# One change in six parts to an encoder block with routed experts: order of small matmuls, one rstd chain, a refill in two halves, a bias moved, stores on two queues

## The chip, the cores and the metric

The kernel runs on one core of one Trainium2 chip. The metric is the device time of one execution in microseconds (us); lower is better. The engines are TensorE (PE, with its weight loads as PEld), VectorE (DVE), ScalarE (ACT), GpSimd (POOL) and SyncE (SP), whose queue issues nearly all transfers.

## The reference, cut to what matters

One layer of an encoder on x (256 tokens, 1024 features, float32). The part around the change is the end of the first sub-layer, the routed experts and the final norm:

```python
x = x + gate1 * (merged @ w_mix_out)                      # this is x1 in the kernel
h = rms_norm(x, norm_ffn_g) * (1 + scale2) + shift2
logits = h @ w_router + b_router                          # 32 experts
top_val, top_idx = lax.top_k(logits, 4); gates = softmax(top_val)
# for each expert e, on its tokens:
gu = h[toks] @ w_gate_up[e] + b_gate_up[e]                # 1024 x 2048
gate = min(gu[:, :1024], 7); up = clip(gu[:, 1024:], -7, 7)
y = ((up + 1) * gate * sigmoid(1.702 * gate)) @ w_down[e] + b_down[e]
x = x + gate2 * sum over the token's 4 experts of gates * y
out = rms_norm(x, final_norm_g)
```

Everything is float32. The weights of the 32 experts are 12 MiB each (8 for gate and up, 4 for down), and all of them are read once.

## The kernel before, in words

The 256 tokens lie as two tiles (t = 0, 1) of 128 rows. Each engine has its own hand-written program, and the engines meet at counting semaphores: an engine's queue is worked off in order, so what stands behind a wait waits too.

**Weights.** A pair is two experts, A and B, of 64 token slots each. It reads twelve blocks of 2 MiB: four for gate and up of A, two for down of A, four for gate and up of B, two for down of B. The blocks go through eleven slots in SBUF in turn (place, L342). SP issues the loads (L403 gate and up, L409 down); before each it waits in free (L434) until PE has counted, on the semaphore consumed, the block that lay in the slot. Fifteen pairs (FIXED) are written out, the last goes through a loop whose count comes from a table (looped_pair), and its last down block is loaded as four halves of 1 MiB (L467). Block 11 of the first pair is the first refill: it goes into slot 0, which held gate-and-up block 0 of the same pair, and waits for that block's count. The three loads ahead of it wait for the mixing matmuls and for x1.

**Between the mixing product and the experts.** On DVE, residual (L1555) makes x1 in five pieces and counts x1_rdy; the last piece is columns 768 to 1023 of tile 1. ACT squares the rows of x1 (L1187). row_rstd (L1574) turns the sums of one tile into 1/sqrt(mean) by a chain of nine small steps, for tile 0 ahead of the last residual piece, for tile 1 at the end. PE turns x1 over (L796), multiplies it with the router weights (L801), puts in the gate-and-up biases (L834), and adds x1 to the accumulators with an identity matrix (add_x1, L829: four matmuls of 512 columns, tiles and halves apart). Three of those stand ahead of the first gather: two before the ranks (L839 to L841), which wait for m01_rdy from DVE, and one after them. DVE answers the ranks with the selection matrices (L1602); PE then gathers the tokens of pair 0 (L854), ACT and DVE scale them (L1205, L1618), and gate_up_block (L892, sixteen records a block) starts. The fourth add_x1 follows the four blocks.

**A pair on PE.** gate_up(A), scatter of the pair before (L923), act_transpose (L904, waits for DVE's activation L1656 to L1660), ACT's copy (L1217), down (L916), gate_up(B), gather of the next pair (L880), down (B). In DVE, y_copy (L1698) scales the product of down and counts y_rdy.

**The end.** After pair 14 comes down_bias (L970: four matmuls of 512 columns with 32 rows), then the looped pair, whose first instruction waits for y_rdy of the pair before; then the last scatter. ACT squares (L1259), DVE multiplies with the final gain (L1803), runs the rstd chain for both tiles (L1811, L1289 to L1297), ACT scales tile 0 (L1263), DVE tile 1 (L1814, L1816), and SP stores the four quarters of the output (L485).

Of the kernel before, what the change touches and what calls it, by code (L numbers as in the profile page):

```python
# [29 lines left out]
ALU = mybir.AluOpType  # L30
# [3 lines left out]
P = 128  # L34
D = 1024
L = 256
TT = L // P
# [63 lines left out]
def build(nc, a, out):  # L101
    with ExitStack() as ctx:
# [39 lines left out]
        NJ, NC = 4, 2  # L142
# [112 lines left out]
        def sem(name):  # L255
# [9 lines left out]
            s_ps s_sb negm_rdy exp_done a_rdy aT_ps aT_sb o_ps o_sq on_rdy oT_ps oT_sb  # L265
            rb_ps rb_sb pj_ps pj_sb gat_rdy mix_ps x1_rdy x2_rdy x1_sq  x1T_ps bc_sb x1T_dve x1T_act exc_sb
            log_ps top_rdy top_exp m_rdy rank_ps cnt_ps cnt_sb ex_ps g_all gt_ps gt_sb tables sel0_rdy m01_rdy ga0_act ga0_dve
            consumed tr_done sc_done ga_done pt_done
            g_rdy sig_rdy act_rdy actT_rdy y_rdy ga_sb pt_sb sel_rdy wt_rdy mask_rdy
            sc_part fin_sq fin_rs fin_act fin_rdy loop_y dve_step act_step dve_loop pool_step""".split()  # L270
        S = {n: sem(n) for n in names}
# [63 lines left out]
        FIXED = E // 2 - 1  # L335
# [28 lines left out]
        def _(sp):  # L364
# [69 lines left out]
            def free(p, i):  # L434
                sp.wait_ge(S["consumed"], used(p, i - NS + 1))
# [34 lines left out]
            def expert_of(index):  # L470
                return sp.value_load(table_i[0:1, bass.ds(index, 1)], min_val=0, max_val=E - 1)

            free(0, DB + 1)
            down(place(0, DB + 1), 1, 1)
            for p in range(1, FIXED):
# [7 lines left out]
            sp.dma_start(fgB, a["final_norm_g"][:].partition_broadcast(P)).then_inc(S["fg_in"], 16)  # L483
            def store(t, h):
                sp.dma_start(out[0, t * P:(t + 1) * P, 512 * h:512 * (h + 1)], fin[:, t, 512 * h:512 * (h + 1)])\  # L485
                    .then_inc(S["out_done"], 16)

            sp.wait_ge(S["fin_act"], 1)
            store(0, 0)
            sp.wait_ge(S["fin_rdy"], 1)  # L490
            store(1, 1)
            sp.wait_ge(S["fin_act"], 2)
            store(0, 1)
            sp.wait_ge(S["fin_rdy"], 2)
            store(1, 0)
            sp.wait_ge(S["out_done"], 16 * TT * 2)

# [11 lines left out]
        def _(pe):  # L509
# [318 lines left out]
            def add_x1(t, h):  # L828
                mm(bank(2 * t + h), ident, x1[:, t, h * 512:(h + 1) * 512], start=True, stop=False, skip_group_check=True)  # L829
# [15 lines left out]
            biases(0)  # L845
            add_x1(1, 0)
            add_x1(1, 1)
            pe.wait_ge(S["m01_rdy"], 1)
            ranks(0, M01).then_inc(S["rank_ps"], 1)
            add_x1(0, 0)  # L850

# [32 lines left out]
            def gate_up_block(p, s, j):  # L884
                w, landed, count = place(p, (A0, B0 if isinstance(p, int) else L_B)[s] + j)
                pe.wait_ge(landed, count)
                for kk in range(2):
                    k = 2 * j + kk
                    for b in range(2):
                        for h in range(2):  # L890
                            o = kk * 2048 + b * 1024 + h * 512
                            last = mm(ps[64 * h:64 * h + 64, 4 + b, :], hTp[:, k, s * 64:(s + 1) * 64],  # L892
                                      w[:, o:o + 512], start=False, stop=(k == KD - 1))
                last.then_inc(S["consumed"], 1)

# [47 lines left out]
            for j in range(NJ):  # L943
# [10 lines left out]
                elif j == 1:  # L954
                    expert_sums()
            pe.wait_ge(S["exc_sb"], 1)
            add_x1(0, 1)

# [27 lines left out]
            def down_b(p):  # L986
                pe.wait_ge(S["ga_sb"], p * 2 + 1)
                pe.wait_ge(S["act_rdy"], p * 2 + 2)
                act_transpose()
                pe.wait_ge(S["actT_rdy"], p * 2 + 2)  # L990
                pe.wait_ge(S["wt_rdy"], p + 1)
                place_weights()
                pe.wait_ge(S["ga_sb"], p * 2 + 2)
                down([place(p, DB + c) for c in range(NC)])

            down_a(0)
            gate_up_b(0)
            down_b(0)

            def pair_of(p):  # L1000
                pe.wait_ge(S["mask_rdy"], p + 1)
                gate_up(p, 0)
                pe.wait_ge(S["y_rdy"], p * 2)
                pe.wait_ge(S["pt_sb"], p)
                scatter()
                down_a(p)
                gate_up_b(p)
                down_b(p)

            for p in range(1, FIXED):  # L1010
                pair_of(p)
            down_bias()

# [35 lines left out]
        def _(act):  # L1049
# [212 lines left out]
            for h in range(2):  # L1262
                A(fin[:, 0, 512 * h:512 * (h + 1)], fin[:, 0, 512 * h:512 * (h + 1)], ACT.Copy, scale=rs[:, 0:1])\  # L1263
                    .then_inc(S["fin_act"], 1)

        @block.vector
        def _(v):
# [304 lines left out]

            def row_rstd(t):  # L1574
                v.wait_ge(S["x1_sq"], 2 * t + 2)
                step(V.tensor_tensor(ss[:, t:t + 1], ss4[:, 2 * t:2 * t + 1], ss4[:, 2 * t + 1:2 * t + 2], ALU.add))
                rstd1(rs[:, t:t + 1], ss[:, t:t + 1], D)

            row_rstd(0)
            residual(1, 768, 256, 5, 5)  # L1580
            columns_in(1, 2)
            row_rstd(1)

# [255 lines left out]
```

## Time and profile before

| what | value |
|---|---|
| three runs | 1218.56, 1224.4, 1225.47 us; median 1224.4 |
| the profiled execution | 1226.03 us; its span in the profile 1224.2 us |
| PE busy | 1135.1 us, 93% of the span |
| DVE busy | 426.7 us, 35% |
| ACT busy | 152.2 us, 12% |
| weights and inputs read | 463.77 MB, 380 GB/s over the span |
| mean granted TensorE clock | 0.987 |
| chain that ended last | PE 70%, DMA 23%, ACT 3%, DVE 2% |

### The profile page before, as it was taken

To read this page: it belongs to the slowest core of one execution; us is meant where nothing else is said; L and a number is where in the kernel's file an instruction comes from. 1 tells how busy PE (TensorE), PEld (TensorE's weight loads), DVE (VectorE), ACT (ScalarE), POOL (GpSimd) and SP (SyncE) were. 2 spreads that over 40 slices of the span, in tenths; PEclk is the share of its full clock that TensorE was granted. 3 is DMA by queue.
4 is the path that set the end of the run, shared out by engine and by line. 5 is a ranking of instruction groups with operands and counts; after the bars stand their busy time and mean duration, and the time that the engine had idled before them with its cause. 6 is when DMAs were issued, how large, how long until landed. Compare 5 with 4: busy or idle time off the path is not lost.

```text
span 1224.2 us, 13305 instructions
## 1 busy us (share of the span) xinstructions
PE 1135.1 (93%) x5383; PEld 525.2 (43%) x5383; DVE 426.7 (35%) x953; ACT 152.2 (12%) x332; POOL 0.6 (0%) x7
## 2 busy tenths in 40 slices
PE   3999999999999999999999999999989898899996
PEld 1588678866333333333333343333333333232332
DVE  3467336524723142331313142331313131313133
ACT  1111132301110101101010111101010101010102
POOL 0000000000000000000000000000000000000000
PEclk9999999997999999999999999999999999999899
DMA  9997953277999999999999999999999999999993
GB/s 339 368 384 300 393 194 116 91 287 284 360 424 429 427 428 429 427 427 428 428 428 428 427 427 427 428 428 428 428 427 428 427 427 427 428 427 429 428 424 128
DMA packets 49055, 465.60 MB, mean 380 GB/s; under 512 B 5466, under 2 KB 6220, under 8 KB 21100
## 3 DMA queue, kind: packets, MB, share of 16 engines
q1 hardware_dynamic: 45592, 461.09, 90.5%
q10 hardware_dynamic: 3412, 3.74, 1.0%
q8 instruction: 42, 0.69, 0.2%
q14 instruction: 9, 0.07, 0.0%
HBM read 463.77 MB, written 1.05 MB: 380 GB/s over the span
## 4 chain that ended last, share of the span: by engine, by line
PE 70%; DMA 23%; ACT 3%; DVE 2%; issue 1%; SPq 0%; ACTq 0%; DVEq 0%
PE ps L892 25%; DMA arena<-in_w_gate_up 22%; PE ps L916 13%; PE ps L621 8%; PE ps L880 5%; PE ps L923 3%; PE ps L748 2%; PE ps L770 2%; PE ps L703 2%; PE ps L834 2%; ACT arena L1224 1%; PE ps L615 1%; ACT arena L1217 1%; PE ps L584 1%; PE ps L669 1%
## 5 line engine op out<-in xcount | busy, mean ns | idle before, releaser
L892 PE MATMUL ps<-arena 128*64 128x512 f32 x2048 | 453.8, 597 | 18.7 <-DMA arena<-in_w_gate_up 18.0
L892 PEld LDWEIGHTS ps<-arena 128*64 128x64 f32 x2048 | 142.7, 137 | 326.3 <-issue 286.6
L916 PE MATMUL ps<-arena 128*64 128x512 f32 x1024 | 228.5, 599 | 10.3 <-ACT arena L1217 10.3
L1656 DVE TENSOR_SCALAR arena<-ps 128x512 f32<-128x512 f32 x32 | 22.1, 691 | 439.6 <-PE ps L892 439.6
L916 PEld LDWEIGHTS ps<-arena 128*64 128x64 f32 x1024 | 71.0, 138 | 146.0 <-issue 132.2
L1213 ACT ACTIVATE arena<-arena 128x512 f32<-128x512 f32 x32 | 20.1, 630 | 747.3 <-DVE arena L1656 747.3
L621 PE MATMUL ps<-arena 128*128 128x256 f32 x448 | 97.7, 379 | 0.0
L621 PEld LDWEIGHTS ps<-arena 128*128 128x128 f32 x448 | 84.9, 190 | 13.9 <-issue 2.6
L1698 DVE TENSOR_TENSOR arena<-ps,arena 64x512 f32<-64x512 f32 x64 | 44.1, 689 | 125.0 <-PE ps L916 124.3
L880 PEld LDWEIGHTS ps<-arena 128*128 128x128 f32 x512 | 58.4, 192 | 12.2 <-issue 12.2
L880 PE MATMUL ps<-arena 128*128 128x128 f32 x512 | 61.4, 278 | 0.0
L923 PE MATMUL ps<-arena 128*128 128x512 f32 x128 | 59.3, 605 | 0.9 <-DVE arena L1698 0.9
L1224 ACT ACTIVATE arena<-ps,arena 128x128 f32<-128x128 f32 x128 | 48.2, 457 | 14.1 <-PE ps L880 14.1
L1684 DVE TENSOR_SCALAR arena<-arena 128x128 f32<-128x128 f32 x128 | 44.2, 346 | 4.2
L923 PEld LDWEIGHTS ps<-arena 128*128 128x128 f32 x128 | 22.9, 189 | 37.0 <-issue 36.5
L834 PE MATMUL ps<-arena 32*64 32x512 f32 x256 | 36.6, 642 | 0.0
L1670 DVE SCALAR_TENSOR_TENSOR arena<-arena 128x128 f32<-128x128 f32 x96 | 33.8, 352 | 3.4
L934 PE MATMUL ps<-arena 128*128 128x128 f32 x32 | 7.0, 300 | 24.3 <-ACT arena L1217 24.3
L1410 DVE SCALAR_TENSOR_TENSOR arena<-arena 128x2048 f32<-128x2048 f32 x12 | 28.2, 2352 | 3.0 <-DMA arena<-in_w_ada 2.6
L703 PE MATMUL ps<-arena 128*128 128x256 f32 x128 | 29.1, 381 | 0.0
L770 PE MATMUL ps<-arena 128*128 128x512 f32 (+1 forms) x80 | 28.0, 507 | 0.0
L748 PE MATMUL ps<-arena 128*128 128x256 f32 x128 | 28.0, 379 | 0.0
(248 smaller groups left out, 624.4 us busy)
## 6 DMA issues: line engine op xcount, KB each, us to landing
arena<-in_w_gate_up SPq DMA_DIRECT2D x128, 2048.0 KB, 37.9
arena<-in_w_down SPq DMA_DIRECT2D x62, 2048.0 KB, 36.1
arena<-in_w_ada SPq DMA_DIRECT2D x12, 2048.0 KB, 17.2
arena<-in_w_in SPq DMA_DIRECT2D x10, 2048.0 KB, 16.3
arena<-in_w_mix_out SPq DMA_DIRECT2D x2, 2048.0 KB, 8.9
arena<-in_w_down SPq DMA_DIRECT2D x4, 1024.0 KB, 41.6
arena<-in_w_hy_out SPq DMA_DIRECT2D x1, 2048.0 KB, 14.8
arena<-in_w_attn_out SPq DMA_DIRECT2D x1, 2048.0 KB, 19.4
```

The lines of the kernel that those rows point to most:

```text
L621: last = mm(bank(b, 256, c * 256), w[:, k, cc * P:(cc + 1) * P], hT[:, k, :], start=(k == 0), stop=(k == KD - 1))
L703: last = mm(bank(m % 3, 256, (i % 2) * 256), w[:, k, cc * P:(cc + 1) * P], hT[:, k, :], start=(k == 0), stop=(k == KD - 1))
L748: last = mm(bank(pj_bank[i % 4], 256, o), w[:, k, i * P:(i + 1) * P], src[:, k, :], start=(k == 0), stop=(k == CT - 1))
L770: return mm(bank(7 if c0 == 768 else 2 * t + c0 // 512, n), merged[:, k, t * P:(t + 1) * P], mix[k // 4][:, k % 4, c0:c0 + n], start=(k == ...
L834: mm(ps[64 * h:64 * h + 64, 4 + b, :], mask[E * b:E * b + E, s, :], sel_bias[E * b:E * b + E, h * 512:(h + 1) * 512], start=True, stop=False)
L880: last = mm(bank(b, 128, kk * 128), xn[:, t, k * P:(k + 1) * P], Sel[:, t, :], start=(t == 0), stop=(t == TT - 1))
L892: last = mm(ps[64 * h:64 * h + 64, 4 + b, :], hTp[:, k, s * 64:(s + 1) * 64], w[:, o:o + 512], start=False, stop=(k == KD - 1))
L916: last = mm(ps[64 * h:64 * h + 64, out_bank, :], lhs, rows[:, qq * D + h * 512:qq * D + (h + 1) * 512], start=(q == 0), stop=(q == 7))
L923: return mm(bank(2 * t + h), Pw[:, t, :], y[:, h * 512:(h + 1) * 512], start=False, stop=stop, skip_group_check=True)
L1224: last = A(hTp[:, k, :], ps[:, 7 - half, kk * P:(kk + 1) * P], ACT.Identity, scale=gs2(k), bias=sh2(k))
L1684: st(V.tensor_scalar(dst[:, t, :], iota, pk[:, k, t:t + 1], gk[:, k, t:t + 1], ALU.is_equal, ALU.mult))
L1698: last = V.tensor_tensor(y[64 * s:64 * s + 64, 512 * h:512 * (h + 1)], ps[64 * h:64 * h + 64, out_bank, :], gate2B[64 * h:64 * h + 64, 512 ...
```

## The change

1. **One rstd chain.** row_rstd for tile 0 and tile 1 is replaced by one chain for both (rstd, twelve steps on two columns) at the end, and the copy of turned columns (columns_in(1, 2)) stands ahead of the last residual piece.
2. **x1 later.** The three add_x1 ahead of the first gather stand behind the four gate-and-up blocks of pair 0; the fourth stands between act_transpose and down.
3. **First refill in two halves.** PE counts half_used after half of block 0; SP loads the first MiB on that, the second on the full count. Down of expert 1 waits for both.
4. **down_bias** stands at the start of pair 12 (the thirteenth) instead of behind pair 14.
5. **Stores.** ACT issues the two of tile 0 from its own queue, SP the two of tile 1.
6. Semaphores renamed or dropped (x2_rdy and pool_step were not waited for).

```diff
@@ -263,11 +263,11 @@
             mc_sb h1_sb h1_act kA_ps kN_ps kB_ps kA_sb kf_done
             u_ps u_sb v_sb vT_rdy vt_ps vt_sb V_ps Y_rdy yT_ps yhy_rdy lam_a lam_e
             s_ps s_sb negm_rdy exp_done a_rdy aT_ps aT_sb o_ps o_sq on_rdy oT_ps oT_sb
-            rb_ps rb_sb pj_ps pj_sb gat_rdy mix_ps x1_rdy x2_rdy x1_sq  x1T_ps bc_sb x1T_dve x1T_act exc_sb
+            rb_ps rb_sb pj_ps pj_sb gat_rdy mix_ps x1_rdy out0_done x1_sq  x1T_ps bc_sb x1T_dve x1T_act exc_sb
             log_ps top_rdy top_exp m_rdy rank_ps cnt_ps cnt_sb ex_ps g_all gt_ps gt_sb tables sel0_rdy m01_rdy ga0_act ga0_dve
             consumed tr_done sc_done ga_done pt_done
             g_rdy sig_rdy act_rdy actT_rdy y_rdy ga_sb pt_sb sel_rdy wt_rdy mask_rdy
-            sc_part fin_sq fin_rs fin_act fin_rdy loop_y dve_step act_step dve_loop pool_step""".split()
+            sc_part fin_sq fin_rs fin_act fin_rdy loop_y dve_step act_step dve_loop half_used half_in""".split()
         S = {n: sem(n) for n in names}
         s_front = [sem(f"front_in{j}") for j in range(6)]
         s_slot = [sem(f"slot_in{k}") for k in range(11)]
@@ -470,8 +470,11 @@
             def expert_of(index):
                 return sp.value_load(table_i[0:1, bass.ds(index, 1)], min_val=0, max_val=E - 1)
 
+            first_again, landed, _ = place(0, DB + 1)
+            sp.wait_ge(S["half_used"], 1)
+            sp.dma_start(first_again[:, 0:2048], w_dn[1, 1][:, 0:2048]).then_inc(S["half_in"], 16)
             free(0, DB + 1)
-            down(place(0, DB + 1), 1, 1)
+            sp.dma_start(first_again[:, 2048:4096], w_dn[1, 1][:, 2048:4096]).then_inc(landed, 16)
             for p in range(1, FIXED):
                 pair_of(p, 2 * p, 2 * p + 1)
             sp.wait_ge(S["tables"], 2)
@@ -481,19 +484,12 @@
             q = sp.value_load(table_i[0:1, 49:50], min_val=E // 2 - 1, max_val=ITEMS // 2 - 1)
             sp.wait_ge(S["consumed"], used(q, NJ))
             sp.dma_start(fgB, a["final_norm_g"][:].partition_broadcast(P)).then_inc(S["fg_in"], 16)
-            def store(t, h):
-                sp.dma_start(out[0, t * P:(t + 1) * P, 512 * h:512 * (h + 1)], fin[:, t, 512 * h:512 * (h + 1)])\
+            for n, h in enumerate((1, 0)):
+                sp.wait_ge(S["fin_rdy"], n + 1)
+                sp.dma_start(out[0, P:2 * P, 512 * h:512 * (h + 1)], fin[:, 1, 512 * h:512 * (h + 1)])\
                     .then_inc(S["out_done"], 16)
-
-            sp.wait_ge(S["fin_act"], 1)
-            store(0, 0)
-            sp.wait_ge(S["fin_rdy"], 1)
-            store(1, 1)
-            sp.wait_ge(S["fin_act"], 2)
-            store(0, 1)
-            sp.wait_ge(S["fin_rdy"], 2)
-            store(1, 0)
-            sp.wait_ge(S["out_done"], 16 * TT * 2)
+            sp.wait_ge(S["out0_done"], 16 * 2)
+            sp.wait_ge(S["out_done"], 16 * 2)
 
 
         @block.gpsimd
@@ -843,11 +839,8 @@
             pe.wait_ge(S["gub_in"], 32)
             pe.wait_ge(S["mask_rdy"], 1)
             biases(0)
-            add_x1(1, 0)
-            add_x1(1, 1)
             pe.wait_ge(S["m01_rdy"], 1)
             ranks(0, M01).then_inc(S["rank_ps"], 1)
-            add_x1(0, 0)
 
             def gather0(t, c):
                 for k in (2 * c, 2 * c + 1):
@@ -884,6 +877,7 @@
             def gate_up_block(p, s, j):
                 w, landed, count = place(p, (A0, B0 if isinstance(p, int) else L_B)[s] + j)
                 pe.wait_ge(landed, count)
+                first = isinstance(p, int) and p + s + j == 0
                 for kk in range(2):
                     k = 2 * j + kk
                     for b in range(2):
@@ -891,6 +885,8 @@
                             o = kk * 2048 + b * 1024 + h * 512
                             last = mm(ps[64 * h:64 * h + 64, 4 + b, :], hTp[:, k, s * 64:(s + 1) * 64],
                                       w[:, o:o + 512], start=False, stop=(k == KD - 1))
+                    if first and kk == 0:
+                        last.then_inc(S["half_used"], 1)
                 last.then_inc(S["consumed"], 1)
 
             def gate_up(p, s):
@@ -953,8 +949,9 @@
                     counts()
                 elif j == 1:
                     expert_sums()
-            pe.wait_ge(S["exc_sb"], 1)
-            add_x1(0, 1)
+            add_x1(1, 0)
+            add_x1(1, 1)
+            add_x1(0, 0)
 
             def expert_weights_turned():
                 pe.wait_ge(S["g_all"], TOPK)
@@ -991,13 +988,22 @@
                 pe.wait_ge(S["wt_rdy"], p + 1)
                 place_weights()
                 pe.wait_ge(S["ga_sb"], p * 2 + 2)
+                if isinstance(p, int) and p == 0:
+                    pe.wait_ge(S["half_in"], 16)
                 down([place(p, DB + c) for c in range(NC)])
 
-            down_a(0)
+            pe.wait_ge(S["act_rdy"], 1)
+            act_transpose()
+            pe.wait_ge(S["exc_sb"], 1)
+            add_x1(0, 1)
+            pe.wait_ge(S["actT_rdy"], 1)
+            down([place(0, DA + c) for c in range(NC)])
             gate_up_b(0)
             down_b(0)
 
             def pair_of(p):
+                if p == FIXED - 3:
+                    down_bias()
                 pe.wait_ge(S["mask_rdy"], p + 1)
                 gate_up(p, 0)
                 pe.wait_ge(S["y_rdy"], p * 2)
@@ -1009,7 +1015,6 @@
 
             for p in range(1, FIXED):
                 pair_of(p)
-            down_bias()
 
             def looped_pair(p):
 
@@ -1262,6 +1267,9 @@
             for h in range(2):
                 A(fin[:, 0, 512 * h:512 * (h + 1)], fin[:, 0, 512 * h:512 * (h + 1)], ACT.Copy, scale=rs[:, 0:1])\
                     .then_inc(S["fin_act"], 1)
+                act.wait_ge(S["fin_act"], h + 1)
+                act.dma_start(out[0, 0:P, 512 * h:512 * (h + 1)], fin[:, 0, 512 * h:512 * (h + 1)])\
+                    .then_inc(S["out0_done"], 16)
 
 
         @block.vector
@@ -1571,15 +1579,12 @@
             columns_in(0, 1)
             residual(1, 512, 256, 4, 4)
 
-            def row_rstd(t):
-                v.wait_ge(S["x1_sq"], 2 * t + 2)
-                step(V.tensor_tensor(ss[:, t:t + 1], ss4[:, 2 * t:2 * t + 1], ss4[:, 2 * t + 1:2 * t + 2], ALU.add))
-                rstd1(rs[:, t:t + 1], ss[:, t:t + 1], D)
-
-            row_rstd(0)
+            columns_in(1, 2)
             residual(1, 768, 256, 5, 5)
-            columns_in(1, 2)
-            row_rstd(1)
+            v.wait_ge(S["x1_sq"], 2 * TT)
+            row_halves = ss4.rearrange("p (t h) -> p t h", t=TT)
+            step(V.tensor_tensor(ss, row_halves[:, :, 0], row_halves[:, :, 1], ALU.add))
+            rstd(rs, ss, D)
 
             for t in range(TT):
                 v.wait_ge(S["log_ps"], TT)
```

## Rows read from the trace of the kernel before

**Rows 1.** The page: GB/s that the transfers moved, in 40 equal slices.

```profile
GB/s 339 368 384 300 393 194 116 91 287 284 360 424 429 427 428 429 427 427 428 428 428 428 427 427 427 428 428 428 428 427 428 427 427 427 428 427 429 428 424 128
```

**Rows 2.** The chain that ended last: start us, us, what.

```profile
360.50 13.88 PE ps L892 x64
...
415.46 13.88 PE ps L892 x64
...
795.77 43.04 DMA arena<-in_w_gate_up
...
1134.75 3.65 PE ps L892 x16
...
1151.71 3.67 PE ps L970 x8
1155.38 1.92 PE ps L834 x8
1157.30 16.23 PE ps L892 x64
```

**Rows 3.** Windows: us, PE, PEld, DVE, ACT, POOL busy, clock, DMA, GB/s.

```profile
284.00:286.00 2.00, 2.00 (x15) 2.00 (x14) 1.41 (x8) 0.32 (x1) 0.00 (x0) 0.69 1.01 434
298.00:300.00 2.00, 1.55 (x10) 1.09 (x10) 0.73 (x2) 0.81 (x2) 0.00 (x0) 0.89 0.00 0
326.00:328.00 2.00, 2.00 (x12) 0.66 (x10) 1.82 (x6) 0.00 (x0) 0.00 (x0) 1.00 0.22 78
328.00:330.00 2.00, 2.00 (x12) 0.60 (x10) 0.93 (x3) 0.00 (x0) 0.00 (x0) 1.00 0.76 180
330.00:1196.00 866.00, 813.80 (x3958) 307.10 (x3954) 252.31 (x565) 82.88 (x186) 0.00 (x0) 1.00 1.01 427
1156.00:1158.00 2.00, 2.00 (x10) 0.29 (x4) 0.00 (x0) 0.00 (x0) 0.00 (x0) 0.50 1.00 426
```

**Rows 4.** The chain of the stretch 276 to 346 us: start us, us, what.

```profile
283.69 3.86 PE ps L801 x24
...
289.46 3.71 PE ps L829 x4
...
294.25 1.92 PE ps L829 x2
296.16 2.49 PE ps L854 x12
...
299.54 3.65 PE ps L892 x16
...
322.29 8.78 PE ps L916 x32
```

**Rows 5.** Timeline around 282 to 321 us, VectorE.

```profile
282.10 0.42 DVE L1559 TENSOR_TENSOR arena<-ps,arena 128x256 f32<-128x256 f32 x1
...
289.96 0.18 DVE L1595 TENSOR_REDUCE arena<-arena 128x4 f32<-128x16 f32 x1
...
320.20 0.69 DVE L1660 TENSOR_TENSOR arena<-arena 128x512 f32<-128x512 f32 x1
```

**Rows 6.** Timeline around the end, VectorE, ScalarE and the queue of SP.

```profile
1151.76 1.40 DVE L1698 TENSOR_TENSOR arena<-ps,arena 64x512 f32<-64x512 f32 x2 [6.60 <-PE ps L916]
...
1216.59 0.16 DVE L1811 TENSOR_TENSOR arena<-arena 128x2 f32<-128x2 f32 x1 [0.17 <-ACT arena L1259]
...
1218.96 1.33 ACT L1263 ACTIVATE arena<-arena 128x512 f32<-128x512 f32 x2 [2.47 <-DVE arena L1297]
...
1219.70 1.82 SPq L485 DMA_DIRECT2D out<-arena  x4
```

**Rows 7.** Line L403, last two issues (1130 to 1135 us), and their landing.

```profile
L403 SPq DMA_DIRECT2D arena<-in_w_gate_up x2: 4035/4038/4042, 1130.7 to 1134.9; - x2
...
DMA to landing us min/median/max: 48.1/48.4/48.7
```

**Rows 8.** The page, transfers: KB each, median us from issue to landing.

```profile
out<-arena SPq DMA_DIRECT2D x4, 256.0 KB, 2.4
```

## Prediction, made before the changed kernel was timed

> **What bounds the kernel now.** I read the page first: from the twelfth slice to the last but one the transfers move 424 to 429 GB/s, whatever PE does, and in slices 6 to 11 they don't [rows 1]. Then the chain of waits: from 795.77 on it goes through the landings of gate and up weights, 43 us and more at a time, and the last block for which PE waits is the one at 1134.75 [rows 2]. Before that PE is ahead of nothing: a pair takes it 54.96 us (415.46 less 360.50 [rows 2]), while its twelve blocks of 2.097 MB take 25.17/0.427 = 58.9 us at the rate of the window 330 to 1196 [rows 3]. So the end is set by two things: **when the transfer stream has its last gap**, and **what PE does after 1134.75**. From there to the last output the chain holds no transfer.
>
> The last gap is at 326 to 329: the stream falls to 78 and 180 GB/s, and from 330 on it is full [rows 3]. Its block waits for the first half of down of expert 0. That product started at 322.29 and took 8.78 us [rows 4]; 32 records cost half of the 13.88 us of 64, 6.94 [rows 2], so 1.84 us are a clock at half speed in the first half: this ended at 322.29 + 8.78 - 3.47 = 327.6, and the stream runs again about 1 us later, at 328.6.
>
> **The change part by part.**
>
> *One rstd chain, and the copy ahead.* The last residual piece started at 282.10 [rows 5], behind the tile 0 chain. Its mixing product is ready when the router matmuls start, about 281.4 (the chain gives 3.86 us of router from 283.69 [rows 4], a transposition before that, and the first four of them earlier); I take 281.45, so 0.65 us. The merged chain costs 1218.96 - 1216.59 = 2.37 us, as the same twelve steps do at the end [rows 6]; it starts with the last squares, about 283.1, and is done at 285.5, over 1 us ahead of the router product, which hides it. If that cover went, up to 0.5 us. The clock falls from full to half near 284.8 (0.69 in 284 to 286 [rows 3]), so work done 0.65 us earlier gets more of the full clock: the router ends at 286.6 and not at 287.55. Term: 0.9 us, bounds 0.6 and 1.0.
>
> *The three add_x1 ahead of the gather.* They cost 3.71 + 1.92 = 5.63 us at half clock [rows 4]. With them gone the ranks wait for DVE instead: m01 was ready at 289.96 + 0.18 = 290.14 [rows 5], now at 289.2, while PE has its biases done at 288.5. The ranks (294.25 less 289.46 + 3.71 = 1.1 us [rows 4]) end at 290.4, DVE needs about 0.7 us for the first selection, and the gather starts at 291.2, where it started at 296.16. Its first three quarters took 2.49 us, part of them at full clock [rows 4]; all at half I take 2.6, and 0.85 for ACT: block 0 starts at 294.7 in place of 299.54, 4.8 us earlier.
>
> What clock does it get? In the rows half speed lasts from 284.8 to 298.4 (0.89 in 298 to 300 [rows 3]), through biases with 32 rows and ranks of two columns, and the rise comes after an add_x1 and 2 us of gather. Now the gather begins sooner, with gaps of 0.7 us before the ranks and before it. I take a rise near 295.3, 0.3 us lost, and 4.5 us gained at block 0. Never worse than a rise at the old 298.4: 1.9 us lost, 2.9 gained; bounds 2.9 and 4.8. The Trainium skill, page "TensorE: Matmul & The Clock Gate", section "A second HAM failure mode: psum-queue depth-cycling", says that small idle times between groups of matmuls make the clock swing between its levels. By that rule the new gaps speak against this part; it is rival B.
>
> *First refill in two halves.* It is asked for 1.8 us (half of 3.65 [rows 4]) before block 0 ends. But the next refill waits for block 1, some 6 us after block 0, and one block takes 4.9 us (2.097/0.427), so the stream runs dry behind it as before. Value nothing at the end. One more issue on SP, 0.46 us (1.82/4 [rows 6]), with nothing queued behind it that is due.
>
> *The add_x1 behind the blocks.* After block 3 PE sat idle for DVE's activation: four steps of 0.7 us, the last done at 320.20 + 0.69 = 320.89 [rows 5]. Three add_x1 at full clock cost 3 x 0.96 (half of 1.92 [rows 4]) = 2.9 us, which is this gap; the fourth lies beside ACT's copy (0.6 us) and sticks out by 0.3. So down starts 4.2 us earlier, at 318.1. And PE is busy where it idled ahead of 322, so the fall to half is gone: down's first half takes 3.5 us and ends at 321.6, against 327.6: **6.0 us earlier**. The stream has its three blocks before that moved at 321.7 at the earliest, so a gap of 1 us stays there, PE still sets it, and the stream is moved by 6.0. Bounds: 2.9 + 1.0 = 3.9 with a late rise, 6.9 if the gap closed.
>
> *down_bias in pair 12.* It costs 3.67 us [rows 2], and the half clock behind it (0.50 in 1156 to 1158 [rows 3]) another 16.23 - 13.88 = 2.35 on the four blocks and 0.96 on the biases [rows 2]: 3.3. In pair 12 PE gains 58.9 - 55.0 = 3.9 us a pair on the stream; over the three pairs to the block of 1134.75 that is 11.8, against 7.0. Hidden, and nothing if the clock stays up. The slots are freed up to 7 us late, but a block lands 48 us after its issue [rows 7], so the stream does not run dry.
>
> At the end it does not bring all of 7.0. The looped pair waits for y_rdy, and DVE's y_copy runs from 1151.76 for 1.40 us [rows 6]; down_bias covered that. Now PE idles until 1153.2 and gains 1155.38 - 1153.2 = 2.2 of the 3.67. The idle time with 1 us of 32-row matmuls is shorter than the 5.6 us of before, so I take the clock to stay full: 2.2 + 3.3 = 5.5 at the end of gate and up of A. What is late next is the stream: the fourth gate-and-up block of B is issued at 1134.9 and lands 48.4 us later [rows 7], at 1183.3, where PE would come at about 1183.8. The blocks of A may hold PE for some tenths. Term: 5.2 us, bounds 1.9 (clock falls) and 5.5.
>
> *Stores.* SP's four issues ran from 1219.70 for 1.82 us, the last begun at 1221.1 [rows 6]. Now ACT works 0.66, issues 0.46, works 0.66, issues: its last begins at 1220.8. Term 0.3 us. No store from ACT stands in the trace; bounds 0.9 better (two queues side by side) and 2.4 worse (one landing more [rows 8]). The nearest row is SP's, hence 0.3.
>
> **Sum:** 6.0 + 5.2 + 0.3 = 11.5 off the profiled execution's 1226.03, 1214.5. That one was 1.6 above the median. Both dips of the clock that I remove were in it in full, which a median run need not have, so I give half of the 1.6 back on the gain: about **1215**.
>
> **Rivals.**
> B. *The clock does not follow.* It rises only after half of block 0, or falls at the wait in front of the looped pair. For it: it fell near 322, after 3 us of little work (the 8.78 of [rows 4]). Against: every pair idles for ACT's copy ahead of down, and the mean from 330 to 1196 is still 1.00 [rows 3]. Price 2 or 3.3 us: about 1218.
> C. *The stream's gap was hidden anyway*, so that only the end counts. For: PE and stream run nearly level for 300 us. Against: the landings in the chain [rows 2]. 1226.0 - 5.5 = 1220.5.
> D. *Slower.* Half speed through the four first blocks: what keeps it there are the new gaps around the ranks and the gather, and the waits of 0.1 to 0.5 us between blocks. Each microsecond at half costs half a microsecond; past the start of block 0 it eats the whole 11.5 + 0.3 when it lasts 24 us, so through the blocks, the add_x1 and down. Then the last gap comes some 8 us later than now, and with the end's gain it is about 1229. Against: the same blocks hold the clock at 1.00 from 330 to 1196 [rows 3].
> That the half refill does nothing is in the forecast.
>
> **How the numbers follow.** Forecast 0.72, B 0.17, C 0.07, D 0.04. A measurement of this kernel can tell about 0.5%, 6.1 us, from no change: faster is under 1218.3. The forecast lies there but for a few hundredths, B for over half; C and the rest of B are within; D is slower: 0.80, 0.16, 0.04. The range takes the forecast's bounds (gap closed and stores at their best: 1212, and 1.6 for the median, 1210.5) and B and most of C above: 1210.5 to 1220.5.
>
> **What the profile would show.** Block 0 starts 4 to 5 us earlier after the mixing product; full clock at the latest in its first half; the last gap of the stream near 322 and not at 328, and under 1.5 us; no clock of 0.5 near 322; PE waits about 1.5 us for DVE's y_copy at the looped pair; the last pair's blocks waiting for transfers by tenths; ACT's second store issued last. Wrong if the last gap has moved by under 4 us, if the clock is at half in the last pair, or if PE comes late to pair 14's last gate-and-up block.

## The result, and the profile after

The changed kernel ran at a median of 1214.0 us (six runs, 1213.06 to 1217.25), the kernel before beside it at 1222.87 us (six runs). The ratio is 0.9927, 95% interval 0.9907 to 0.9948, so 0.7% less; held against before once more it was 0.9941 (0.9921 to 0.9962), and its 13 runs together have a median of 1214.07 us. The forecast was 1215.0 us in 1210.5 to 1220.5. One execution of the kernel before took 1740.81 us at a mean clock of 0.653 and is left out of every number here.

The page of the changed kernel, GB/s in 40 slices (before in [rows 1]):

```profile
span 1212.3 us, 13300 instructions
...
GB/s 340 363 396 306 392 202 103 107 270 349 366 425 429 427 427 429 426 428 427 428 427 429 427 428 427 428 428 428 427 428 428 427 428 427 428 427 428 427 426 201
```

The stream is full from the twelfth slice on, as before, and at the same rate. So nothing was gained in the 840 us in between; the differences lie at both ends of it. The chain of the changed kernel (start us, us, what), from the window 272 to 330 us, and below it its last part:

```profile
276.42 1.73 PE ps L766 x8
...
293.36 4.78 PE ps L886 x16
...
317.41 7.02 PE ps L912 x32
```

```profile
1127.93 3.65 PE ps L886 x16
...
1144.94 0.58 DVE arena L1703
1145.77 0.56 DVE arena L1703
1146.38 1.09 PE ps L830 x8
1147.47 13.89 PE ps L886 x64
...
1166.45 14.07 PE ps L886 x64
```

The rows to hold against [rows 2, 4]: down of expert 0 took 7.02 us and not 8.78, block 0 (L886) began at 293.36 and not 299.54, the last block PE waits for in pair 15 at 1127.93 and not 1134.75, and from there to the end of the span it is 84.4 us and not 89.5. The wait for y_copy stands in the chain as the two L1703. Together that is 6.8 + 5.1 = 11.9 us of span. Of the 6.8 us, 1.1 are an earlier start of the mixing product's last part (276.42; in the profile of before this record is `277.50 1.74 PE ps L770 x8`), which no changed line touches. In the windows (us, PE, PEld, DVE, ACT, POOL busy, clock, DMA, GB/s) the last gap, at 326 to 330 before [rows 3], is now here:

```profile
320.00:322.00 2.00, 2.00 (x12) 0.69 (x10) 1.79 (x7) 0.00 (x0) 0.00 (x0) 1.00 0.62 250
322.00:324.00 2.00, 2.00 (x12) 0.58 (x8) 1.80 (x6) 0.00 (x0) 0.00 (x0) 1.00 1.00 262
```

### The profile page after: what moved, and what is told of

It is laid out like the page before. It is cut to its first block, busy times and chain, and to the rows that moved or that the text cites. A ratio compares the mean times of both kernels' runs of the same rounds, so it can differ in the third digit from the quotient of the medians.

```text
span 1212.3 us, 13300 instructions
## 1 busy us (share of the span) xinstructions
PE 1126.3 (93%) x5383; PEld 523.5 (43%) x5383; DVE 425.6 (35%) x947; ACT 152.1 (13%) x332; POOL 0.6 (0%) x7
## 4 chain that ended last, share of the span: by engine, by line
PE 73%; DMA 21%; ACT 3%; DVE 1%; SPq 1%; issue 1%; ACTq 0%; DVEq 0%
PE ps L886 27%; DMA arena<-in_w_gate_up 18%; PE ps L912 14%; PE ps L617 8%; PE ps L873 5%; PE ps L919 3%; DMA arena<-in_w_ada 2%; PE ps L744 2%; PE ps L766 2%; PE ps L699 2%; PE ps L830 2%; ACT arena L1229 1%; PE ps L611 1%; ACT arena L1222 1%; PE ps L665 1%
## 5 line engine op out<-in xcount | busy, mean ns | idle before, releaser
L886 PE MATMUL ps<-arena 128*64 128x512 f32 x2048 | 452.8, 598 | 14.3 <-DMA arena<-in_w_gate_up 14.3
L886 PEld LDWEIGHTS ps<-arena 128*64 128x64 f32 x2048 | 143.4, 138 | 319.7 <-issue 288.2
L1703 DVE TENSOR_TENSOR arena<-ps,arena 64x512 f32<-64x512 f32 x64 | 44.1, 689 | 123.4 <-PE ps L912 122.7
L1689 DVE TENSOR_SCALAR arena<-arena 128x128 f32<-128x128 f32 x128 | 44.2, 345 | 4.1
L766 PE MATMUL ps<-arena 128*128 128x512 f32 (+1 forms) x80 | 28.0, 507 | 0.0
## 6 DMA issues: line engine op xcount, KB each, us to landing
arena<-in_w_ada SPq DMA_DIRECT2D x12, 2048.0 KB, 17.8
```

What stands on the lines that cost most here:

```text
L766: return mm(bank(7 if c0 == 768 else 2 * t + c0 // 512, n), merged[:, k, t * P:(t + 1) * P], mix[k // 4][:, k % 4, c0:c0 + n], start=(k == ...
L1689: st(V.tensor_scalar(dst[:, t, :], iota, pk[:, k, t:t + 1], gk[:, k, t:t + 1], ALU.is_equal, ALU.mult))
L1703: last = V.tensor_tensor(y[64 * s:64 * s + 64, 512 * h:512 * (h + 1)], ps[64 * h:64 * h + 64, out_bank, :], gate2B[64 * h:64 * h + 64, 512 ...
```

## Experiments

Twelve runs were made: eleven variants or repeats, each timed in five rounds with the kernel before beside it, and one execution of the kernel before that was profiled again. The ratio given is to the kernel before of the same rounds, with its 95% interval. The run to run spread of this kernel is large (before, in 90 runs beside the experiments: 1217.1 to 1226.6 us, median 1221.9), so the profiles carry the argument and the ratios bound it.

**Where the spread comes from.** `before_again` is the kernel before, without an edit, profiled once more.

> The kernel before, profiled once more. Its unprofiled runs spread over 1217.8 to 1226.5 us with mean clocks from 0.994 down to 0.987. Theory (the spread is TensorE's clock at a few places): where this profile has a higher mean clock than the first, it has no half clock behind the idle stretch at 319 us or at the looped pair, and its span is shorter by half of the missing half-clock time, while all other durations agree. Rival: the spread comes from transfers, and the rate from 330 us on differs.

It had a mean clock of 0.990 and a span of 1223.7 us, against 0.987 and 1224.2. Its chain:

```profile
279.20 1.74 PE ps L770 x8
...
299.67 3.65 PE ps L892 x16
...
322.42 8.62 PE ps L916 x32
```

```profile
1134.19 3.65 PE ps L892 x16
...
1154.78 1.71 PE ps L834 x8
1156.49 16.54 PE ps L892 x64
```

The expectation missed in its main point and held for the rest. Both half clocks were there again (down at 8.62, gate and up of the last pair at 16.54 us); the higher mean came from the half clock ahead of block 0, 10.2 us of it and not 13.7, and from a full clock at the start. From the mixing product (279.20; 277.50 before) to block 0 it took 20.5 us and not 22.0, yet the span is only 0.5 us shorter, since the mixing product itself came 1.7 us later. So two things vary from run to run: the start of the mixing product (275.8 to 279.2 us in the profiles of this study, before any changed line), and the places where the clock is at half. The 90 runs of before go with their mean clocks:

| mean granted clock | runs | median us |
|---|---|---|
| 0.994 and over | 15 | 1218.1 |
| 0.992 and 0.993 | 14 | 1219.9 |
| 0.991 | 20 | 1221.6 |
| 0.989 and 0.990 | 27 | 1224.5 |
| under 0.989 | 14 | 1224.5 |

The stream's rate was the same: 428 GB/s over 340 to 1180 in both profiles.

**The front alone.** `e1_front`: the merged chain and the moved add_x1; refill, down_bias and stores as before.

```diff
-            add_x1(1, 0)
-            add_x1(1, 1)
             pe.wait_ge(S["m01_rdy"], 1)
             ranks(0, M01).then_inc(S["rank_ps"], 1)
-            add_x1(0, 0)
...
-            pe.wait_ge(S["exc_sb"], 1)
-            add_x1(0, 1)
+            add_x1(1, 0)
+            add_x1(1, 1)
+            add_x1(0, 0)
```

> The kernel before with the two front parts alone (one rstd chain, add_x1 moved); the refill stays whole, down_bias and the stores stay. Theory (the end follows the last gap of the transfer stream): the gap moves from about 328 to about 322, the last landing PE waits for moves with it, and the time is 5 to 6 us below before; the end path keeps its 3.67 us of down_bias and its half clock. Rival (the stream was hidden, only the end path counts): within 1 us of before, though the gap moves.

Median 1217.93 us, ratio 0.9971 (0.9952 to 0.9989). Its chain, the second part with down_bias still behind pair 15:

```profile
276.18 1.73 PE ps L770 x8
...
293.97 3.65 PE ps L889 x16
...
316.90 7.02 PE ps L913 x32
```

```profile
1127.43 3.65 PE ps L889 x16
...
1144.39 3.63 PE ps L968 x8
1148.01 1.02 PE ps L834 x8
1149.03 13.88 PE ps L889 x64
```

The landing that PE waits for moved to 1127.43: the stream is not hidden, and the rival falls. The gain in the median is 3.5 to 4 us and not 5 to 6. The profile on which I worked it out had 13.7 us of half clock ahead of block 0, and `before_again` 10.2, so that it needed 1.8 us more from the mixing product to down than the second. And the end path surprises: here down_bias stands where it stood, and the clock stays up, 13.88 us and not 16.23. The half clock in that place is not a fixed cost of down_bias.

**add_x1 without the merged chain.** `e5_addx1_only`, the edit above alone.

> The kernel before with add_x1 moved and nothing else. Theory: add_x1 is nearly all of the front part, the merged rstd chain with the copy ahead brings 0.6 to 1 us: within 1 us slower than the run with both. Block 0 of pair 0 starts about 0.7 to 1 us later after the mixing product than there. Rival (without the merged chain the ranks wait for it and the front gains nothing): same as before.

Median 1221.87 us, ratio 0.9983 (0.9963 to 1.0003): not told apart from before by time, so only the profile speaks against the rival. The chain:

```profile
276.09 1.74 PE ps L770 x8
...
295.26 4.34 PE ps L889 x16
...
318.88 7.02 PE ps L913 x32
```

From mixing to block 0 it is 19.2 us, against 16.9 to 17.8 in nine profiles with both edits. Like with like is the profile of `e1_front`, where the clock fell to half as soon behind the mixing product (7 us) as here: 17.8 us, so the merged chain is worth 1.4 us at block 0 and not 0.6 to 1. In these two profiles one half of that is the wait for VectorE ahead of the last turned columns (0.83 and 0.17 us), and the other half the last 24 router records, of which more ran at half clock (4.34 and 3.62 us). In the five profiles with 16.9 us the clock fell later, 8.8 us or more behind the mixing product, so the rest of the 2.2 us is not shown to be the chain's. At the half of down `e5_addx1_only` is 46.3 us behind the mixing product and `e1_front` 44.2 (the table further down). That is 2.1 us, but 0.7 of them are half clock that ran on into block 0 here (4.34 and not 3.65 us). Against the first profile of before, with 13.7 us at half clock ahead of down like this one, the moved add_x1 brought 50.1 - 46.3 = 3.8 us.

**down_bias alone.** `e2_bias13`, the kernel before with down_bias at the start of the thirteenth pair.

```diff
             def pair_of(p):
+                if p == FIXED - 3:
+                    down_bias()
...
-            down_bias()
```

> The kernel before with down_bias in the thirteenth pair alone. Theory: the last gap of the stream stays near 328, PE waits about 1.5 us for y_copy at the looped pair, the clock stays at 1.00 there, and the time is 4 to 5.5 us below before. Rival (down_bias is not hidden in pair 13, PE comes late to the last block of pair 15): 0 to 2 us below before. Rival (the clock falls at the wait as well): 2 us below.

Median 1219.42 us, ratio 0.9979 (0.9959 to 0.9999). The chain:

```profile
1134.47 3.65 PE ps L892 x16
...
1151.48 0.58 DVE arena L1699
...
1152.93 1.09 PE ps L834 x8
1154.02 15.58 PE ps L892 x64
```

The last block waited for stands at 1134.47, as in before: the matmuls are hidden in the thirteenth pair. In this profile the wait for y_copy was followed by half clock, 15.58 us and not 13.88, and the gain in the median, 2.4 us, is that of the second rival and not the 4 to 5.5 of the theory. So both forms of the end occur with and without it.

**down_bias too late to hide.** `e8_bias_pair15`, the changed kernel with the condition `p == FIXED - 1`.

> The changed kernel with down_bias at the start of pair 15 (index 14) instead of pair 13. Theory (PE gains 3.9 us a pair on the stream and needs over one pair to take up 3.7 us plus up to 3.3 of half clock): PE comes to the last block of pair 15 0 to 3 us late, and the time is 0 to 3 us above the changed kernel, more in executions with a low mean clock. Rival (a pair hides all of it): same time.

Median 1217.81 us, ratio 0.9966 (0.9947 to 0.9984), some 3 us above the changed kernel. From here on its chain holds no landing any more:

```profile
1085.69 4.04 PE ps L967 x8
1089.72 1.91 PE ps L830 x8
1091.64 15.87 PE ps L886 x64
```

From the half of down to the end of the span this profile takes 896.1 us, the profiles of `e2_bias13` and `e3_old_stores`, with half clock in the last pair as here, 892.9 and 893.0. One pair is not enough for 3.7 us and the half clock behind it; three are. In the changed kernel's own profile the same place, in pair 13, is followed by 15.35 us of gate and up, and in its repeat by 6.8 us of half clock, and PE waits for transfers again before the end in both.

**The idle stretch.** `e7_gap_idle`: the changed kernel with the three add_x1 behind down of expert 0.

```diff
-            add_x1(1, 0)
-            add_x1(1, 1)
-            add_x1(0, 0)
...
             down([place(0, DA + c) for c in range(NC)])
+            add_x1(1, 0)
+            add_x1(1, 1)
+            add_x1(0, 0)
             gate_up_b(0)
```

> The changed kernel, but the three add_x1 stand behind down of expert 0, so that PE idles again for 3 us while VectorE activates; block 0 starts as early as in the changed kernel. Theory (busy PE keeps the clock up there): in some executions the clock is 0.50 for 3 to 4 us behind the idle stretch, the last gap of the stream comes up to 1.8 us later and the time is 0.5 to 2 us above the changed kernel, with the lower mean clocks going with the longer times. Rival (the fall near 322 in the kernel before had nothing to do with the idle stretch): clock at 1.00 there and the same time.

Median 1218.64 us, ratio 0.9963 (0.9947 to 0.9980). Windows, same columns as above:

```profile
316.00:318.00 2.00, 0.00 (x0) 0.00 (x0) 1.93 (x3) 0.59 (x1) 0.00 (x0) 1.00 1.01 434
318.00:320.00 2.00, 1.84 (x6) 1.15 (x6) 1.83 (x6) 0.60 (x1) 0.00 (x0) 0.58 0.99 418
320.00:322.00 2.00, 2.00 (x6) 0.44 (x6) 1.81 (x6) 0.00 (x0) 0.00 (x0) 0.57 1.01 434
...
324.00:326.00 2.00, 2.00 (x12) 0.58 (x10) 1.79 (x7) 0.00 (x0) 0.00 (x0) 1.00 0.20 61
...
336.00:338.00 2.00, 2.00 (x12) 0.69 (x10) 0.00 (x0) 0.00 (x0) 0.00 (x0) 1.00 0.99 270
```

PE idles at 316 to 318 and the clock is at half behind it, as in both profiles of before; in every profile with add_x1 in that place (ten of them) it is at 1.00. The price was higher than I expected, about 4 us. One reason is in the last line: the three matmuls now stand ahead of gate and up of B, the slots behind come free later, and the stream has a second gap at 336 to 338. What the rest of it is I did not separate.

**The half refill and the stores.** `e4_whole_refill` and `e3_old_stores` take one of these parts each out of the changed kernel: SP waits for the whole of block 0 and loads 2 MiB at once; SP issues all four stores.

> The changed kernel with the first refill in one transfer. Theory (the half refill is swallowed by the next gap): same time as the changed kernel, last gap at the same place relative to down of expert 0. Rival (the earlier start of the stream counts): 1 to 2 us slower than the changed kernel.

> The changed kernel with the stores of before (all four from SP). If two queues save what the forecast gave them, this is 0.3 us slower than the changed kernel; the profile of the changed kernel (5.33 us from the end of the rstd chain to the end of the span, 5.24 before) says 0 to 0.1 us faster. Either way the difference lies below what the rounds can tell, so the stretch behind the rstd chain in the profile decides.

Medians 1214.98 and 1216.09 us, ratios 0.9949 (0.9931 to 0.9967) and 0.9946 (0.9928 to 0.9964). To know what that means, the changed kernel was timed again in rounds of its own:

> The changed kernel once more with the rounds of the other runs, since the variants that came out 0.5% below before (old stores, whole refill, late halves, the two fillings) were held against six runs of it taken elsewhere. Theory (those edits are worth nothing, and the spread is the clock's and the start's): 1213 to 1217.5 us, median 1214.5 to 1215.5, ratio to before 0.993 to 0.996, that is the same as theirs. Rival (the whole refill or the old stores cost 1 to 2 us): median at or below 1214.0 and a ratio of 0.993.

1214.78 us (1213.56 to 1219.42), ratio 0.9941 (0.9921 to 0.9962): no part is told apart. Two of the seven runs, 1219.02 and 1219.42, lie above the range that I had expected. For the refill the profile agrees: with the whole transfer block 0 started 16.9 us behind the mixing product, as in the changed kernel, and the half of down came 43.4 us behind it and not 44.5, the difference being the 1.1 us of half clock in the changed kernel's block 0, which this execution did not have. For the stores the stretch behind the rstd chain decides. The changed kernel's timeline (start us, us, engine or its queue, line):

```profile
1206.97 0.72 ACT L1268 ACTIVATE arena<-arena 128x512 f32<-128x512 f32 x1 [2.47 <-DVE arena L1305]
...
1207.72 0.39 ACTq L1271 DMA_DIRECT2D out<-arena  x1
1207.75 0.83 SPq L489 DMA_DIRECT2D out<-arena  x2
1208.16 0.72 ACT L1268 ACTIVATE arena<-arena 128x512 f32<-128x512 f32 x1 [0.47 <-ACT arena L1268]
1208.91 0.36 ACTq L1271 DMA_DIRECT2D out<-arena  x1
```

and its transfers on the page:

```profile
out<-arena ACTq DMA_DIRECT2D x2, 256.0 KB, 2.9
out<-arena SPq DMA_DIRECT2D x2, 256.0 KB, 2.9
```

The last store is issued 1208.91 - 1206.97 = 1.9 us behind the chain and not 2.1 [rows 6], but ACT stood 0.47 us for its own issue, and a store lands in 2.9 us and not 2.4 [rows 8]. From the end of the chain to the end of the span it is 5.3 us against 5.2 in before, and 5.3 in the profile of `e3_old_stores` too, whose four stores from one queue landed in 2.4 us: 1214.8 less 1209.5.

**Two attempts at more.** `e9_late_halves`: block 3 of the second pair, the one behind the last gap, in two halves too (PE counts late_used after the first two of four parts of down block 0, and waits for both halves; of its edit only SP's part is shown).

```diff
+                    if p == 1 and j == 3:
+                        dst, landed, _ = place(1, 3)
+                        sp.wait_ge(S["late_used"], 1)
+                        sp.dma_start(dst[:, 0:2048], w_gu[e_a, 3][:, 0:2048]).then_inc(S["late_in"], 16)
+                        free(1, 3)
+                        sp.dma_start(dst[:, 2048:4096], w_gu[e_a, 3][:, 2048:4096]).then_inc(landed, 16)
+                        continue
...
```

> The changed kernel, and the fourth refill behind the first (block 3 of pair 1, the one behind the last gap) in two halves as well, the first asked for after half of down block 0. Theory (the last gap sets the stream): the gap near 321 closes or falls under 0.3 us, and the time is about 1 us below the changed kernel. Rival (the changed kernel is now bound by PE in the last pair, which waits there for transfers by 0.2 us): same time.

Median 1214.97 us, ratio 0.9952 (0.9934 to 0.9970): a miss. Windows of half a microsecond around the old gap:

```profile
322.50:323.00 0.50, 0.50 (x4) 0.14 (x2) 0.43 (x3) 0.00 (x0) 0.00 (x0) 1.00 1.31 442
323.00:323.50 0.50, 0.50 (x6) 0.21 (x4) 0.46 (x2) 0.00 (x0) 0.00 (x0) 1.00 0.65 180
323.50:324.00 0.50, 0.50 (x6) 0.21 (x4) 0.43 (x3) 0.00 (x0) 0.00 (x0) 1.00 1.04 147
324.00:324.50 0.50, 0.50 (x6) 0.15 (x3) 0.47 (x2) 0.00 (x0) 0.00 (x0) 1.00 1.58 197
324.50:325.00 0.50, 0.50 (x4) 0.14 (x2) 0.46 (x2) 0.00 (x0) 0.00 (x0) 1.00 0.32 131
```

The first half was issued at 321.50, 1.5 us ahead of the end of the traffic before it, and the queue never fell silent; still it ran at 131 to 197 GB/s for two microseconds. Over 322 to 326 the stream moved 299 and 221 GB/s, so it lacked (129 + 207) x 2/428 = 1.6 us of its 428 GB/s, as much as the changed kernel lacks over 320 to 324 (178 + 166, 1.6 us). Why the restart is slow although the issue came early, I have not found.

`e10_wait_filled` and `e11_ranks_filled` give PE work in two waits: matmuls of an identity matrix whose product is not used in the wait for y_copy, and one add_x1 too many (the same values again) ahead of the ranks.

```diff
+            pe.wait_ge(S["pt_sb"], FIXED)
+            mm(bank(7), ident, x1[:, 0, 0:512], start=True, stop=True)
+            mm(bank(7, 256), ident, x1[:, 0, 0:256], start=True, stop=True)
```

```diff
             biases(0)
+            add_x1(1, 0)
             pe.wait_ge(S["m01_rdy"], 1)
```

> The changed kernel with two matmuls of an identity matrix on 128 rows (512 and 256 columns, their product is not used) in PE's wait for y_copy ahead of the looped pair. Theory (idle PE and biases of 32 rows bring the clock down there in some executions): no execution profiled has half clock behind the looped pair's start; executions of the changed kernel at 1216 to 1217 us go, the best stay at 1213 to 1214, median 0 to 1 us lower. Rival (the biases alone bring it down): half clock there as before, times the same.

> The changed kernel with one add_x1 more (it is done again later, so nothing changes in the product) in PE's wait ahead of the ranks. Theory: at full clock it fits into the gap of 1.6 us and the fall to half comes later or not at all, block 0 starts up to 1 us earlier after the mixing product (16.9 to 17.8 us in the changed kernel); where the clock has fallen before, it costs 0.3 us. Rival (the fall is due to the router's 32-column matmuls, before this gap): no gain, up to 0.3 us slower.

Medians 1215.82 and 1215.3 us, ratios 0.9955 (0.9937 to 0.9974) and 0.9956 (0.9941 to 0.9970): no gain. With the second the add_x1 ran into the half clock and took 2.00 us, and block 0 began 296.30 - 279.02 = 17.3 us behind the mixing product. In the changed kernel's profile, where the clock fell about as late (9.0 us behind it, 8.7 here), it is 16.9, so this cost 0.3 us, as the rival said. The first had full clock in the last pair, but so had four of nine profiles with the wait empty; its runs spread over 1212.6 to 1217.4 us, no less than the changed kernel's. No version beat the changed kernel.

## Why the prediction was right

**What bounds the kernel** held, and eleven profiles give it as a number. In this table the first column is the start of the eight records of the mixing product in the chain (L770, L766; of two such groups the first), the next the end of the first half of down of expert 0 (its start and 3.5 us, or its end less 3.5 where the clock fell), then the last block of pair 15 for which PE waited for a landing; all three in us from the start of the span, and after them the differences:

| kernel | mixing | down, half | landing | half - mixing | landing - half | span - half | half clock in last pair |
|---|---|---|---|---|---|---|---|
| before | 277.5 | 327.6 | 1134.8 | 50.1 | 807.2 | 896.6 | yes |
| before_again | 279.2 | 327.5 | 1134.2 | 48.3 | 806.7 | 896.2 | yes |
| e5_addx1_only | 276.1 | 322.4 | 1129.9 | 46.3 | 807.5 | 897.0 | yes |
| e1_front | 276.2 | 320.4 | 1127.4 | 44.2 | 807.0 | 893.2 | no |
| e2_bias13 | 279.0 | 327.4 | 1134.5 | 48.4 | 807.1 | 892.9 | yes |
| e3_old_stores | 277.7 | 321.8 | 1129.0 | 44.1 | 807.2 | 893.0 | yes |
| e9_late_halves | 278.6 | 323.1 | 1130.5 | 44.5 | 807.4 | 891.7 | no |
| e10_wait_filled | 278.9 | 323.4 | 1130.9 | 44.5 | 807.5 | 891.8 | no |
| e4_whole_refill | 276.6 | 319.9 | 1127.5 | 43.4 | 807.6 | 892.0 | no |
| changed kernel | 276.4 | 320.9 | 1127.9 | 44.5 | 807.0 | 891.4 | no |
| after_again | 275.8 | 319.8 | none | 44.0 | | 891.9 | no |
| e11_ranks_filled | 279.0 | 323.5 | 1131.5 | 44.5 | 808.0 | 893.8 | yes |

The landing follows the half of down by 806.7 to 808.0 us, whatever was changed: the last gap sets the stream, and the time is that plus a front and an end. In `after_again` PE did not wait at that block but six blocks on, for one that came 837.0 us behind the half of down; less six blocks of 4.9 us that is 807.6. Two profiles are not in the table: `e8_bias_pair15`, where PE came too late to wait, and `e7_gap_idle`, whose stream had the second gap.

**The front.** Forecast 6.0 us, from 50.1 to 44.1; measured 50.1 - 44.5 = 5.6 against the first profile and 48.3 - 44.5 = 3.8 against the second. That the first agrees better is luck: it had 3.4 us more of half clock ahead of block 0 than the second, and the edits are not shown to be what shortens that. The mechanisms held: the idle stretch in front of down took the add_x1, the half clock near 322 went, the gap moved to 321 to 324. It lacked 1.6 us of its rate there, a little over the 1.5 I had named. The merged chain was undersized (0.9 forecast with a bound of 1.0, 1.4 measured between `e5_addx1_only` and `e1_front`). The clock came back where I put it, near 295 to 296, in the first half of block 0, and cost 4.78 - 3.65 = 1.1 us there, not 0.3.

**The half refill** is worth nothing, as costed: with the whole transfer the half of down was no later (43.4 us, 44.5 with the half clock of block 0 put in). The next gap is at 304 to 306 in the changed kernel.

**down_bias.** That three pairs hide it and one does not held. The wait for y_copy was there: 1146.38 less the end of down at 1144.91 is 1.5 us, as forecast. The end gained 896.6 - 891.4 = 5.2 us, the term of the sum to a tenth, against that profile. But the sum took the half clock as the effect of down_bias and as gone with it, and this step was wrong: e1_front has down_bias in the old place and full clock, e2_bias13 and e3_old_stores have it moved and half clock. Like with like, from that landing to the end of the span, it is 86.2 - 84.4 = 1.8 us where the clock stays up (`e1_front` and the changed kernel), forecast as 2.2, and 89.5 - 85.8 = 3.7 us where it falls (before, and `e2_bias13`, `e3_old_stores` and `e11_ranks_filled`). That is part of rival B, which the prediction gave 0.17 and priced at 3.3 us: the clock fell behind the wait in five of nine profiles with down_bias moved and the wait left empty, and cost 15.58 - 13.88 = 1.7 us in gate and up. By the prediction's own sign, half clock in the last pair, these five would have counted against it; the two profiles of the changed kernel itself do not show it.

**The stream in the last pair** was named as the next thing to come late, at the fourth block of B. The changed kernel's L886 x64 of 14.07 us has 0.2 us of waiting in it, and in its repeat that block stands in the chain behind a landing:

```profile
1165.47 10.45 PE ps L886 x48
1176.31 3.65 PE ps L886 x16
```

(1176.31 less the end of the three blocks at 1175.92 is 0.4 us).

**The stores** were costed at 0.3 us and brought nothing: the last issue is 0.2 us earlier, the landing takes 0.5 us more.

**The sum** was 11.5 us off the profiled execution's 1226.03; the changed kernel's profiled execution took 1214.07, 12.0 less. That they agree so well is in part luck, since 1.1 of the 12.0 us are the mixing product's start. Against the medians it is 8.9 us, 9.4 forecast. The last step of the working does not follow, though: 11.5 off an execution that was 1.6 above the median, with half of the 1.6 given back, is a gain of 10.7 on the median of 1224.4 and so 1213.7, not 1215. Nor does the 8 us of rival D follow from its 24 us at half clock, which cost 12: that puts the gap 6 us later than before. Neither slip decides the outcome, for both 1213.7 and 1215 lie within 1 us of the measured 1214.0.

That the gain differs so between profiles and medians I put down to the clock: before in its 15 best runs (mean clock 0.994 and over) had a median of 1218.1, the changed kernel in its five such runs 1213.6, a gain of 4.5; between the medians of all runs it is 1221.9 - 1214.1 = 7.8. From this I estimate that some half of the gain is waiting that was taken away, and the other half is half clock that comes less often. These are runs sorted by their mean clock, on several chips, and no execution of before with a clock of 0.994 was profiled, so the split is an estimate and not shown.

**The Trainium skill's** rule in "TensorE: Matmul & The Clock Gate", "A second HAM failure mode: psum-queue depth-cycling", would have made the new small gaps a loss. The profiles show it in part: half clock ran on through the gather and into block 0 (4.78 us and not 3.65 in the changed kernel), but the stretch at half was 10.2 us long, as in `before_again` and shorter than the 13.7 of the first profile. Over all profiles with the new gaps it was 10.2 us in nine, 13.7 in `e5_addx1_only` and 6.8 in `e4_whole_refill`; in the three without them 13.7, 10.2 and 10.2. So they do not show that the gaps lengthened it, and PE came out ahead.

## What to carry to other kernels

Where a transfer stream is full for most of a kernel, look for its last gap, and price an edit ahead of it by how far it moves the work that the gap waits for. Small matmuls cost their full time where the engine would otherwise go on to that work, and nothing in a stretch where it idles anyway. An edit whose worth is a half clock that went has to be priced over several profiles, since in one the clock may have fallen by chance. Work moved out of the end uncovers what it had covered: look at the first instruction behind it for a wait.

## What was not expected of the hardware

- The clock at the same place of the same program is at half in one execution and full in another: behind PE's wait for y_copy it fell in five profiles (e2, e3, e7, e8, e11) and stayed at 1.00 in four (the changed kernel and its repeat, e4, e9). The 90 runs of before are ordered by their mean clocks, over 6.4 us from the highest class to the lowest two; that it is these few places is argued from the profiles and not shown run by run.
- The stream restarted slowly where it had nearly run dry: 131 to 197 GB/s for 2 us in `e9_late_halves`, although the next transfer had been issued 1.5 us ahead, so halving that transfer closed no gap. The cause is open.
- Stores on two queues at once landed in 2.9 us each, four on one queue in 2.4.
